# A transformer and state-space stack on one core: table clusters with longer products, and fewer slabs in two halves

## The chip, the cores and the metric

The kernel runs on one core of a Trainium2 chip. The metric is the device time of one execution in microseconds. Three runs of the kernel before took 3143.59 to 3145.2 us, with a median of 3145.1 us.

## The reference

The input is one sequence of 256 tokens of width 2048, in fp32. It goes through two blocks.

The first block has two layers. Each layer computes `h = rms_norm(x) * (1 + scale) + shift`, a token mixer (a chunkwise mLSTM beside a sliding-window attention, with an input projection and an output projection), and a squared-ReLU feed-forward:

```
def squared_relu_mlp(h, w_up, w_down):
    return jnp.square(jax.nn.relu(h @ w_up)) @ w_down
```

`w_up` is 2048 x 8192 and `w_down` is 8192 x 2048. Shift, scale and gate come from `silu(c) @ w_ada`, which has its own 2 x 2048 x 12288 weights.

The second block has a state-space layer (S5) and an attention layer with forget gates. The S5 layer needs tables that depend on its parameters alone: powers of the complex decay of every one of 128 groups of 16 channels with 64 states, multiplied with the output matrix C and the input matrix B. The scan over 256 tokens is then done four tokens at a time, with small matrices `C A^n B` inside the four. Those tables are computed while the second feed-forward of the first block runs.

## The kernel before, in words

**Slabs.** All large products are cut into slabs. A slab is 128 output columns of a weight matrix, 2048 x 128, or 1 MB of fp32, that is 16 chunks of 128 x 128. SyncE loads it into one of five raw buffers. ScalarE makes the high part of the weights (`WH`, rounded to fp32r), VectorE the low part (`WL`, the raw weights minus the high ones). The activations are kept in the same way as a high and a low part of 256 columns each.

TensorE's `slab` (from line 450) does 16 chunks of high weights and then 16 chunks of low weights:

- In **one-form** (the slab's number is in `ONE`, line 164) each chunk of high weights is multiplied with the high and with the low activations, as two products of 256 columns into the same 256 columns of the bank. With the 16 low products that makes 48 products of 256 columns. One instruction evicts the result.
- In **two-half form** nine of the 16 chunks (`WIDE`) take both activation parts in one product of 512 columns, into both halves of the bank. The others are as in one-form. That makes 23 high products (9 of them of 512 columns) and 16 low ones. ScalarE copies the second half out and VectorE adds the first to it.

`IN_TWO` (line 161) is a list of slabs which are taken out of `ONE`. Both forms compute the same sums. Results go to three banks in turn (`BANK_OF`).

**Order.** Every engine has its own program with its instructions in a fixed order, and semaphores join them. The slabs run in one sequence through the whole kernel. A slab waits for its high weights (`s_hi`), for its bank (`s_ev`), and between the high and the low products for its low weights (`s_free`).

**Feed-forward.** The feed-forward of a layer is 128 slabs, here counted from 0 to 127 from `J_MLP[l]` on: four times 16 up slabs and 16 down slabs. Slabs 0 to 2 (`SIDE`) are done apart, as plain fp32 products. In the kernel before, slabs 3 and 4 and the slabs 8, 24, 40, ..., 120 are in two halves in both layers. In the first layer VectorE also multiplies 82 tiles of `w_ada` during slabs 4 to 110. TensorE does nothing but slabs there.

**Table clusters.** In the second layer `s5_tables` (from line 758) puts small work on TensorE behind some slabs: six transposes behind slab 22, and twelve clusters behind slabs 40, 43, 46, 49, 56, 59, 62, 65, 72, 75, 78 and 81. A cluster is 32 fp32 products of 32 columns. They are grouped by `i` (four) and `ri` (the real, then the imaginary part), and in each group four products, `w` = 0 to 3, use four separate strips of 32 columns of the array. The trace shows every fp32 product as two instructions, so a cluster is a row of x64. ScalarE copies the first 128 columns of the bank out. The list `TABLES` (line 160) holds all thirteen places, and in the kernel before the two slabs behind each are in two halves.

Of the kernel before, what the change touches and what calls it, by code (L numbers as in the profile page):

```python
# [56 lines left out]
J_MLP = [53, N_LAYER + 53]  # L57
# [10 lines left out]
def down_slab(l, j, n):  # L68
    return J_MLP[l] + 32 * j + 16 + n
# [33 lines left out]
SIDE = 3  # L103
# [52 lines left out]
for _j in range(N_SLABS):  # L156
# [1 line left out]
    HI_AT.append(_n)  # L158
TAKEN = {_j for _t in TURNS[:-1] for _j in range(_t + 16, _t + 16 + SIDE)}
TABLES = [22] + [40 + 16 * _n + 3 * _g for _n in range(3) for _g in range(4)]  # L160
IN_TWO = ({J_MLP[_l] + _m for _l in range(2) for _m in [SIDE, SIDE + 1] + list(range(8, 128, 16))}
          | {J_MLP[1] + _m + _i for _m in TABLES for _i in (1, 2)}
          | {_t + _n for _t in (J_OUT[0], J_OUT[1], J_Z, J_GLU, J_Y2, J_Y3) for _n in (1, 6, 11)} | {J_OUT[1] + 2})
ONE = (set(range(RAMP)) | {_j for _l in range(2) for _j in range(J_OUT[_l] + 1, J_MLP[_l])}
       | {_j for _l in range(2) for _j in range(J_MLP[_l] + SIDE, J_MLP[_l] + 128)}
# [1 line left out]
       | set(range(J_Z + 2, J_GLU)) | set(range(J_GLU + 1, J_Y2 + 1)) | set(range(J_Y2 + 2, J_KV))  # L167
       | set(range(J_KV + 5, J_KV + 18)) | set(range(J_FOX + 23, J_Y3 + 1)) | set(range(J_Y3 + 2, N_SLABS))) - IN_TWO
DOWN = {down_slab(_l, _p, _n) for _l in range(2) for _p in range(4) for _n in range(16)}
# [26 lines left out]
def build(nc, d, out):  # L196
    ctx = ExitStack()
    with ctx:
# [34 lines left out]
        def m(name, shape, off, dt=F32):  # L233
            return at(name, shape, int(M + off * kb), dt)
# [78 lines left out]
        CC = m("cc", (64, 2, 32), 64)  # L313
        KST = m("kst", (16, 32), 62)
        CP = [m(f"cp{i}", (32, 16), 80 + 2 * i) for i in range(3)]
        BTG = m("btg", (4, 2, 128), 86)
# [109 lines left out]
        def tensor(e):  # L426
            release = {}

            def claim(b):

                if b in release:
                    e.wait_ge(release[b][0], release[b][1])
                return BK[b]

            def mm(o_, l_, r_, start, stop):
                return e.matmul(o_, l_, r_, start=start, stop=stop, skip_group_check=True)  # L436

            def tr(o_, i_):
                n = i_.shape[0]
                return e.transpose(o_, i_, ident[0:n, 0:n])  # L440
# [269 lines left out]
            def layer(l):  # L710
# [29 lines left out]
                for j in range(4):  # L740
                    for n in range(16):
                        if j or n >= SIDE:
                            slab(up_slab(l, j, n), hx, h_chunk(2 * l) if j == 0 and n == SIDE else None)
                        if l == 1:
                            s5_tables(32 * j + n)

                    def raised(k):
                        e.wait_ge(s_uh, 64 * l + 16 * j + k + 1)
                        e.wait_ge(s_ul, 64 * l + 16 * j + k + 1)

                    for n in range(16):
                        slab(down_slab(l, j, n), lambda k: HB[:, k, :, :], None if n else raised)
                        if l == 1:
                            s5_tables(32 * j + 16 + n)
# [3 lines left out]
            def s5_tables(m):  # L758

                if m == 22:  # L760
                    e.wait_ge(s_pd5, 4)
                    for b, cols in ((3, (cs, sn, a2r, a2i)), (4, (a3r, a3i))):
                        bank = claim(b)
                        for i, c in enumerate(cols):
                            last = tr(bank[0:64, 128 * i:128 * i + 128], c)
                        last.then_inc(s_att, 1)
                        release[b] = (s_atr, b - 2)
                for n in range(3):
                    for g in range(4):
                        if m == 40 + 16 * n + 3 * g:  # L770
                            u = 4 * n + g
                            bank = claim(3)
                            e.wait_ge(s_cb, n + 1)
                            e.wait_ge(s_bt, 16 * (u + 1))
                            for i in range(4):
                                for ri in range(2):
                                    for w in range(4):
                                        rows = slice(32 * w, 32 * w + 32)
                                        last = mm(bank[rows, 32 * i:32 * i + 32], BTG[:, i, ri, rows],
                                                  CC[:, 16 * g + 4 * i + w, ri, :], ri == 0, ri == 1)  # L780
                            last.then_inc(s_k0m, 1)
                            release[3] = (s_k0, u + 1)

# [2086 lines left out]
```

## Time and profile before

| | |
|---|---|
| median of three runs | 3145.1 us |
| span of the profiled execution, first to last instruction (the profile gives no other time of it) | 3145.5 us |
| TensorE products | 26577 instructions, busy 3075.0 us |
| TensorE weight loads | busy 2931.5 us |
| VectorE busy | 2404.3 us |
| ScalarE busy | 1529.5 us |
| mean granted TensorE clock | 0.992 |

Products overlap in the array. A product of 256 columns has a duration of about 0.28 us in the trace, but the next starts about 0.11 us later. So the time that a product costs is read from the distance between starts, and a row's "us" (from the first start to the last end of a group) is longer than the distance to the next row.

### The profile page before, as it was taken

Reading aid. Unit: us, or ns where it says so; the run is one execution under the profiler, and the core shown is the slowest. Engines: PE = TensorE matmul, PEld = TensorE weight load, DVE = VectorE, ACT = ScalarE, POOL = GpSimd, SP = SyncE. Lnnn points to the kernel's source line nnn. Section 1 sums busy time; section 2 is a strip of 40 time slices with the busy share of each in tenths; the row PEclk is TensorE's granted clock in tenths of the full one; section 3 lists DMA queues with packets and bytes.
Section 4 is the critical chain, followed back from the end, with each engine's and each line's share of the span. In section 5 each row is a group of like instructions: output and inputs, shape, how many; then the busy total and the mean of one; then the engine's idle time right before and its main releaser. Section 6 shows DMA issues by size and latency. Waiting matters only on the chain.

```text
span 3145.5 us, 61783 instructions
## 1 busy us (share of the span) xinstructions
PE 3075.0 (98%) x26577; PEld 2931.5 (93%) x26577; DVE 2404.3 (76%) x2964; ACT 1529.5 (49%) x2232; POOL 0.2 (0%) x4
## 2 busy tenths in 40 slices
PE   5999999999999999999999999999999999999999
PEld 3889999999999988989999999999899999999998
DVE  7898999788888788776887666687688767556764
ACT  2465664343434556666534444445433556434454
POOL 0000000000000000000000000000000000000000
PEclk7999999999999999999999999999999999999999
DMA  9888869999999745665688666895555554654453
GB/s 409 337 301 331 318 254 349 346 334 350 337 339 342 254 163 212 218 225 175 231 298 307 221 223 240 283 303 202 217 181 189 215 190 158 213 179 159 148 188 121
DMA packets 137025, 791.05 MB, mean 251 GB/s; under 512 B 20081, under 2 KB 38641, under 8 KB 46001
## 3 DMA queue, kind: packets, MB, share of 16 engines
q1 hardware_dynamic: 119714, 769.33, 67.2%
q10 hardware_dynamic: 17040, 17.76, 1.6%
q8 instruction: 211, 3.46, 0.4%
q14 instruction: 60, 0.49, 0.0%
HBM read 769.28 MB, written 17.76 MB: 250 GB/s over the span
## 4 chain that ended last, share of the span: by engine, by line
PE 53%; DVE 2%; ACT 1%; issue 0%; ACTq 0%; DVEq 0%
PE bk L436 52%; DVE wl L1649 1%; PE bk L440 0%; ACT wh L949 0%; DVE pr L1649 0%; DVE Hst L1649 0%; DVE xl L1649 0%; DVE ss L1649 0%; DVE qa L1657 0%; DVE p L1649 0%; DVE X L1649 0%; DVE raw L1657 0%; ACT ln L949 0%; DVE hg L1657 0%; ACT rsy L949 0%
## 5 line engine op out<-in xcount | busy, mean ns | idle before, releaser
L1649 DVE TENSOR_TENSOR wl<-raw,wh 128x2048 fp32r<-128x2048 f32 (+1 forms) x481 | 1092.5, 2271 | 321.1 <-ACT wh L949 318.1
L436 PE MATMUL bk<-HX,wh 128*128 128x256 f32 (+1 forms) x8058 | 1105.8, 294 | 1.8 <-ACT wh L949 1.6
L949 ACT ACTIVATE wh<-raw 128x2048 fp32r<-128x2048 f32 x477 | 911.8, 1912 | 351.1 <-PE bk L436 322.7
L436 PEld LDWEIGHTS bk<-HX,wh 128*128 128x128 f32 x8058 | 1022.2, 188 | 53.4 <-ACT wh L949 2.4
L436 PE MATMUL bk<-HX,wl 128*128 128x256 f32 x4560 | 569.0, 277 | 5.2 <-DVE wl L1649 5.2
L436 PEld LDWEIGHTS bk<-HX,wl 128*128 128x128 f32 x4560 | 542.3, 188 | 7.1 <-DVE wl L1649 7.0
L436 PE MATMUL bk<-hb,wh 128*128 128x256 f32 (+1 forms) x3916 | 488.0, 282 | 0.1
L436 PEld LDWEIGHTS bk<-hb,wh 128*128 128x128 f32 x3916 | 468.2, 188 | 8.2 <-issue 0.3
L1657 DVE SCALAR_TENSOR_TENSOR raw<-raw,cb 128x2048 f32<-128x2048 f32 x192 | 437.5, 2283 | 14.8 <-DMA raw<-in_w_ada 14.7
L436 PE MATMUL bk<-hb,wl 128*128 128x256 f32 x2048 | 253.8, 276 | 0.0
L436 PEld LDWEIGHTS bk<-hb,wl 128*128 128x128 f32 x2048 | 242.5, 188 | 0.0
L949 ACT ACTIVATE ur<-bk 128x256 f32<-128x256 f32 x122 | 46.8, 383 | 354.5 <-PE bk L436 338.4
L436 PE MATMUL bk<-sq,raw 128*128 128x257 f32 (+1 forms) x544 | 119.3, 379 | 0.0
L436 PEld LDWEIGHTS bk<-sq,raw 128*128 128x128 f32 x544 | 102.7, 189 | 17.4 <-issue 1.7
L949 ACT ACTIVATE yt<-bk 128x256 f32<-128x256 f32 x81 | 31.0, 383 | 164.8 <-PE bk L436 157.1
L436 PE MATMUL bk<-hf,rampw 128*128 128x256 f32 x256 | 65.6, 423 | 34.3 <-ACT hf L949 28.8
L436 PEld LDWEIGHTS bk<-hf,rampw 128*128 128x128 f32 x256 | 54.5, 215 | 45.4 <-issue 17.3
L1657 DVE SCALAR_TENSOR_TENSOR ur<-ur 128x256 f32<-128x256 f32 x122 | 51.6, 423 | 45.1 <-ACT ur L949 43.8
L1649 DVE TENSOR_TENSOR tacc<-tacc,ts 128x768 f32<-128x768 f32 (+1 forms) x84 | 72.5, 863 | 2.6 <-ACT yu L949 1.9
L436 PE MATMUL bk<-mx,wh 128*128 128x256 f32 (+1 forms) x483 | 64.8, 285 | 2.2 <-DVE mx L1649 2.1
L436 PE MATMUL bk<-ax,wh 128*128 128x256 f32 (+1 forms) x460 | 65.6, 294 | 0.1
L436 PEld LDWEIGHTS bk<-mx,wh 128*128 128x128 f32 x483 | 60.8, 188 | 4.7 <-ACT mx L949 2.1
(313 smaller groups left out, 2584.1 us busy)
## 6 DMA issues: line engine op xcount, KB each, us to landing
raw<-in_w_ada SPq DMA_DIRECT2D x192, 1024.0 KB, 6.9
raw<-in_w_up SPq DMA_DIRECT2D x128, 1024.0 KB, 6.5
raw<-in_w_down SPq DMA_DIRECT2D x128, 1024.0 KB, 5.7
raw<-in_w_in SPq DMA_DIRECT2D x66, 1024.0 KB, 5.3
raw<-in_kv_w SPq DMA_DIRECT2D x33, 1024.0 KB, 4.9
raw<-in_w_out SPq DMA_DIRECT2D x32, 1024.0 KB, 5.4
raw<-in_s_w_in SPq DMA_DIRECT2D x32, 1024.0 KB, 4.9
raw<-in_fox_w_in SPq DMA_DIRECT2D x32, 1024.0 KB, 4.8
```

The costliest lines, as they stand in the source:

```text
L436: return e.matmul(o_, l_, r_, start=start, stop=stop, skip_group_check=True)
L949: return e.activation(o_, i_, f, **kw)
L1649: return e.tensor_tensor(o_, a_, b_, op)
L1657: return e.scalar_tensor_tensor(o_, a_, s_, b_, op0, op1, accum_out=sums)
```

## The change

Two things are changed. In each of the twelve table clusters the four products of the last group's real part (`i == 3`, `ri == 0`) get `PAST[u]` more columns, 0 to 16, where `u` is the number of the cluster. The added columns are read from the imaginary part, which lies next in `CC`, and are written into columns of the bank that nobody reads.

`IN_TWO` gets shorter. In the first feed-forward slabs 8, 24, ..., 120 are no longer in two halves (slabs 3 and 4 still are). In the second feed-forward slabs 40, 56, 72 and 88 and the two slabs behind each of the twelve clusters are no longer in two halves. Slabs 3, 4, 8, 23, 24, 104 and 120 stay. So 8 and 28 slabs change to one-form.

```
 TABLES = [22] + [40 + 16 * _n + 3 * _g for _n in range(3) for _g in range(4)]
-IN_TWO = ({J_MLP[_l] + _m for _l in range(2) for _m in [SIDE, SIDE + 1] + list(range(8, 128, 16))}
-          | {J_MLP[1] + _m + _i for _m in TABLES for _i in (1, 2)}
+PAST = [0, 1, 2, 3, 4, 5, 6, 7, 8, 10, 12, 16]
+IN_TWO = ({J_MLP[_l] + _m for _l in range(2) for _m in [SIDE, SIDE + 1]}
+          | {J_MLP[1] + _m for _m in [*range(8, 40, 16), 104, 120]}
+          | {J_MLP[1] + TABLES[0] + _i for _i in (1, 2)}
           | {_t + _n for _t in (J_OUT[0], J_OUT[1], J_Z, J_GLU, J_Y2, J_Y3) for _n in (1, 6, 11)} | {J_OUT[1] + 2})
...
                                         rows = slice(32 * w, 32 * w + 32)
-                                        last = mm(bank[rows, 32 * i:32 * i + 32], BTG[:, i, ri, rows],
-                                                  CC[:, 16 * g + 4 * i + w, ri, :], ri == 0, ri == 1)
+                                        n_ = 32 + (PAST[u] if i == 3 and ri == 0 else 0)
+                                        cc = CC[:, 16 * g + 4 * i + w, :, :].rearrange("p r n -> p (r n)")
+                                        last = mm(bank[rows, 32 * i:32 * i + n_], BTG[:, i, ri, rows],
+                                                  cc[:, 32 * ri:32 * ri + n_], ri == 0, ri == 1)
```

## Rows read from the trace of the kernel before

**Rows 1.** The page: busy time of each engine, and the chain that ended last.

```profile
PE 3075.0 (98%) x26577; PEld 2931.5 (93%) x26577; DVE 2404.3 (76%) x2964; ACT 1529.5 (49%) x2232; POOL 0.2 (0%) x4
...
PE 53%; DVE 2%; ACT 1%; issue 0%; ACTq 0%; DVEq 0%
```

**Rows 2.** Busy by stretch: us, PE, PEld, DVE, ACT, POOL (x), PEclk, DMA, GB/s.

```profile
487.93:1140.90 652.97, 652.97 (x5690) 650.00 (x5689) 534.20 (x501) 283.97 (x287) 0.00 (x0) 1.00 0.87 322
1717.92:2079.31 361.39, 361.39 (x3591) 348.54 (x3589) 242.62 (x261) 158.76 (x165) 0.00 (x0) 1.00 0.74 251
2128.88:2168.45 39.57, 39.57 (x338) 39.57 (x337) 30.57 (x31) 21.21 (x28) 0.00 (x0) 1.00 0.58 199
```

**Rows 3.** Timeline of TensorE, second feed-forward: start us, us, operation, [idle before].

```profile
1970.49 3.79 PE L436 MATMUL bk<-hb,wh 128*128 128x256 f32 x32
...
1992.25 3.81 PE L436 MATMUL bk<-hb,wh 128*128 128x512 f32 x23
```

**Rows 4.** Timeline of TensorE, second feed-forward, last down slabs.

```profile
2128.88 3.93 PE L436 MATMUL bk<-hb,wh 128*128 128x256 f32 x32
2132.64 2.05 PE L436 MATMUL bk<-hb,wl 128*128 128x256 f32 x16
...
2168.45 3.82 PE L436 MATMUL bk<-hb,wh 128*128 128x512 f32 x23
```

**Rows 5.** Timeline of TensorE, first feed-forward, slabs 5 to 8.

```profile
473.66 2.15 PE L436 MATMUL bk<-HX,wl 128*128 128x256 f32 x16 [0.30 <-DVE wl L1649]
476.51 4.04 PE L436 MATMUL bk<-HX,wh 128*128 128x256 f32 x32 [0.70 <-ACT wh L949]
480.39 2.05 PE L436 MATMUL bk<-HX,wl 128*128 128x256 f32 x16
...
487.93 3.82 PE L436 MATMUL bk<-HX,wh 128*128 128x512 f32 x23
491.59 1.98 PE L436 MATMUL bk<-HX,wl 128*128 128x256 f32 x16
```

**Rows 6.** Timeline of TensorE, first slab of the S5 output projection.

```profile
2559.42 0.47 PE L436 MATMUL bk<-go,wh 128*128 128x256 f32 x2 [0.84 <-DVE go L1649]
2559.73 2.05 PE L436 MATMUL bk<-go,wl 128*128 128x256 f32 x16
```

**Rows 7.** Timeline of TensorE, third and fourth table cluster.

```profile
1758.27 0.76 PE L436 MATMUL bk<-cc,btg 128*32 128x32 f32 x64
1758.96 4.01 PE L436 MATMUL bk<-HX,wh 128*128 128x512 f32 x23
...
1764.70 3.82 PE L436 MATMUL bk<-hb,wh 128*128 128x512 f32 x23
...
1770.17 3.79 PE L436 MATMUL bk<-hb,wh 128*128 128x256 f32 x32
...
1775.70 0.76 PE L436 MATMUL bk<-cc,btg 128*32 128x32 f32 x64
```

**Rows 8.** Timeline of TensorE, behind the sixth table cluster.

```profile
1833.08 3.92 PE L436 MATMUL bk<-hb,wh 128*128 128x512 f32 x23
1836.84 1.98 PE L436 MATMUL bk<-hb,wl 128*128 128x256 f32 x16
```

**Rows 9.** Timeline of TensorE, third stage, slabs between state products.

```profile
2421.78 4.04 PE L436 MATMUL bk<-HX,wh 128*128 128x256 f32 x32
...
2427.63 0.86 PE L436 MATMUL bk<-u,ks 32*32 32x192 f32 x24
...
2429.45 3.90 PE L436 MATMUL bk<-HX,wh 128*128 128x256 f32 x32
...
2435.09 0.86 PE L436 MATMUL bk<-u,ks 32*32 32x192 f32 x24
```

**Rows 10.** Timeline of TensorE, first layer: 16 plain fp32 products of 256 columns.

```profile
223.50 7.07 PE L436 MATMUL bk<-hf,raw 128*128 128x256 f32 x32
230.41 0.82 PE L440 MATMUL bk<-cst,ta 128*128 128x128 f32 x6
```

## The prediction

> **What bounds the kernel now.** The page comes first: TensorE is busy for 98% of the span and holds 53% of the chain that ended last, with VectorE at 2% and ScalarE at 1% [rows 1]. The busy times by stretch come next: in the first feed-forward (487.93 to 1140.90) TensorE is busy for 652.97 of 652.97 us at the full granted clock (2.4 GHz), VectorE for 534.20 and ScalarE for 283.97 [rows 2]; in the stretch of the table clusters (1717.92 to 2079.31) it is busy throughout as well. So the question is not what waits, but how far apart TensorE starts its products.
>
> That is read from the timeline of TensorE. A slab is one row "wh" (high products) and one row "wl" (16 low products); the distance between two "wh" starts is the slab's time. In one-form (48 products of 256 columns) there are two distances and nothing between them, called the short and the long pace below (and a slab, or a cluster's exit, is short or long by the pace that it runs at or leaves). Short: 1970.49 to 1992.25 is four slabs, 5.44 us each, 113.3 ns a product; the rows read 3.79 and 1.98 [rows 3, 5]. Long: 2128.88 to 2168.45 is seven slabs, 5.653 us each, 117.8 ns a product; the rows read 3.93 and 2.05 [rows 4]. The granted clock is 1.00 in the stretch of long pace as in the others, so this is not the throttle [rows 2]. The price of the long pace is 0.213 us a slab.
>
> The pace is kept until something changes it, and the timeline shows what does:
> - A stop inside a one-form slab leaves it at the long pace. In the first feed-forward slab 5 waits 0.30 us for its low half and slab 6 0.70 us for its high half; the low half of slab 6 then reads 2.05 [rows 5]. The second feed-forward repeats this, and a wait of 0.84 us at 2559.42 is followed by 2.05 too [rows 6]. I count ten slabs of this form with such a stop in the trace; all ten go on at the long pace.
> - A two-half slab (its row is 128x512, x23) ends it: slab 8 at 487.93 has a low half of 1.98 [rows 5], and the one at 2168.45 ends the long pace [rows 4]. At the short pace such a slab takes 5.46 to 5.47, 0.02 to 0.03 more than one-form.
>
> **The change part by part.**
>
> *First feed-forward, slabs 8, 24, ..., 120 go to one-form.* Slabs 3 and 4 stay two-half, but the stops in slabs 5 and 6 come behind them, so slab 8 is the one that restores the pace today. Nothing ahead of it changes: the same loads, high and low halves and waits end at the same times, so slab 8 is reached at the long pace. From there to the end of the stage TensorE never stops today [rows 2], it runs no products but the slabs', and a TensorE that runs later makes stops rarer. I find nothing that would end the long pace: the most slabs in a row at the long pace without a stop or a two-half slab in the trace are the seven between 2128.88 and 2168.45 (and the slab of the stop ahead of it), ended only by the two-half slab [rows 4]. Sum: 120 slabs of 5.653 is 678.4 us, against 652.97 now [rows 2]: +25.4 us. If the pace were short anyway: 120 of 5.44 is 652.8, -0.2 us. These are the two ends; I take the first, its stops and its recovery both being rows of this very place.
>
> *The evictions of the 36 slabs that change form (8 and 28).* One-form needs one eviction where two-half needs a ScalarE copy and a VectorE add. That frees some 0.4 us of ScalarE a slab and costs nothing: both engines have slack in the stretch [rows 2], and a bank is reused three slabs, over 16 us, later. Were that cover gone, a late eviction would be a stop of a few tenths. No instruction waits on anything new, and no load, high or low half changes its place in a queue, SP's included.
>
> *Table clusters.* In slabs 40 to 103 of the second feed-forward twelve clusters stand, three slabs apart, with seven slabs behind the fourth and the eighth, and twenty-two (to the two-half slab 104 that stays) behind the last: 63 slabs that run at the pace that the cluster before them leaves. Today: 361.39 us for the 64 slabs [rows 2]. One cluster's pattern is 0.69 us for the cluster (1758.27 to 1758.96), 5.74 for the two-half slab behind it, at the long pace, 5.47 for the second two-half slab, short again, and 5.53 for the slab ahead of the next cluster, 0.09 over 5.44 [rows 7]. Ten of twelve exits are of this kind; the first and the sixth (3.76 us from 1833.08 to 1836.84, low half 1.98, so 5.57) come out short [rows 8]. So today the clusters' aftermath costs 10 x 0.33 + 2 x 0.16 + 4 x 0.02 (slabs 40, 56, 72, 88) = 3.7 us over 64 x 5.44 + 12 x 0.78 = 357.5; the sum, 361.2, meets the window within 0.2.
>
> After: exits go into one-form slabs. What such an exit costs is seen behind the state product of the third stage: a long exit is 5.85 us (2421.78 to 2427.63), a short one 5.64 (2429.45 to 2435.09), both with 0.09 ahead of the next cluster [rows 9], so 0.10 for the entry and the pace on top. The longer products: a column of an fp32 product of 256 takes 6.91 / 16 / 256 = 1.69 ns (223.50 to 230.41) [rows 10]; the twelve lengths sum to 74 columns, four products side by side, so 74 x 1.69 ns = 0.13 us in all. Base: 357.5 + 12 x 0.10 + 0.13 = 358.8. To it comes 0.213 for every slab behind a long exit.
> - All short: 358.8, -2.5 us. All long: 358.8 + 63 x 0.213 = 372.3, +10.9 us.
> - Whether 1.7 to 27 ns more at the cluster's end turn an exit, no row says. For long: 10 of 12 exits today, and of 27 one-form slabs that come behind products of another kind 24 read long. For short: rows 9 hold one kind of cluster with two different exits, so small shifts do decide. I take nine of twelve long, nearest to these counts: 47 slabs, 10.0 us, +7.5 us.
>
> Two rules of the Trainium skill stand against this, and the sums above do without them. "TensorE: Matmul & The Clock Gate", section "Back-to-back issue gap", gives a gap of N/2.4 + 2.5 ns: 109 ns at 256 columns and 216 at 512, whatever ran before. By it removing a two-half slab loses 9 x 2.5 ns and the first feed-forward would change by +0.2 us in place of +25.4; the trace shows two paces at one size and one clock, 113.3 and 117.8 ns [rows 3, 4], so I weigh it only as the rival without memory. "TensorEngine Tiling (Array Packing)", section "Instruction Overhead", says that a free dimension of 1 costs as much as one of 60. By it 33 to 48 columns are the same as 32 and the exits stay as today's, about 10 of 12 long; the fp32 row's 1.69 ns a column [rows 10] is no test of sizes that small.
>
> **Sum.** +25.4 + 7.5 = +32.9 us. The profiled execution has a span of 3145.5 us, 0.4 over the median of the three runs, 3145.1; the differences are between stretches of this one execution and are put on the median: 3178.0 us.
>
> **Rivals.**
> 1. Most clusters exit short (up to a third long), the first feed-forward stays long: +25.4 and -2.5 to +4: 3168 to 3174. For it: the two short exits today. Against: 24 of 27.
> 2. The pace heals by itself. This is the one on the other side. Its place is slab 8: if the long pace lasts only some slabs behind a stop, and no two-half slab is needed, the first feed-forward gives -0.2 us and the clusters -2.5 to +4: 3142.5 to 3149, not slower. It decides as long as fewer than 6.3 / 0.213 = 30 of the 183 slabs at stake are long. Against it: seven full slabs of unchanged 5.653 us [rows 4].
> 3. The first feed-forward short (slab 5's or 6's stop lands differently and slab 7 is short already), the clusters long: -0.2 and +7.5 to +10.9: 3152 to 3156. Against: ten stops of ten.
> 4. Something turns the pace midway through the first feed-forward, say where up goes over to down products: about +12.7 and +7.5: 3165.
>
> **How the numbers follow.** Forecast (first feed-forward long throughout, half or more of the clusters long, 3174 to 3182): 0.60. Rival 1: 0.20. Rival 2: 0.09. Rival 3: 0.07. Rival 4: 0.04. A difference under 0.2%, 6.3 us, can't be told from none here. Slower: 0.60 + 0.20 + 0.07 + 0.04 = 0.91; same: 0.08 of rival 2; faster: 0.01 of it. The range 3162 to 3184 holds the forecast, rivals 1 and 4 and the bounds of the cluster term, 3168.0 and 3181.4, with some 2.5 us for a new stop at the upper end. Its lower end stops short of rivals 2 and 3.
>
> **What would show it.** Right: from slab 8 at 487.93 on the low rows read 2.04 or 2.05, high rows 3.93, starts 5.653 apart, up to the stage's sums about 25 us later than 1140.90; slabs 5 to 7 as today. Behind each cluster the pace is one of the two and stays it to the next cluster. Slab 104 restores it. Wrong: rows of 1.98 behind 487.93 in one-form; a third pace, or a pace that drifts; a long slab that turns short with no two-half slab, stop or cluster between; or the time moving in another stage, since nothing outside these two stretches should change by over 0.3 us.

## The result, and the profile of the changed kernel

The changed kernel takes 3188.4 us (median; 3189.2, 3189.6, 3187.6, and one execution of 3160.3), the kernel before 3145.2 beside it: ratio 1.0117, interval 1.0097 to 1.0137. It is slower, as forecast, but by 43 us and not by 33, and so 4.4 us above the upper end of the range, 3184. The ratio counts all four executions, the low one too: by it the changed kernel takes about 3182 us, which is inside the range.

The profiled execution has a span of 3187.4 us against 3145.5, +41.9. On the page TensorE is busy for 38.6 us more [rows 1], with 324 more products (9 for each of the 36 slabs that changed form) and as many weight loads:

```profile
PE 3113.6 (98%) x26901; PEld 2984.1 (94%) x26901; DVE 2390.1 (75%) x2929; ACT 1524.0 (48%) x2215; POOL 0.2 (0%) x4
```

Where it went, by stretches between the starts of the blocks of sums of squares (sq, raw), in us:

| stretch | before | changed | difference | forecast |
|---|---|---|---|---|
| start to first block | 436.7 | 434.0 | -2.7 | 0 |
| first feed-forward | 708.5 | 733.95 | +25.4 | +25.4 |
| mixer of the second layer | 347.2 | 347.3 | +0.1 | 0 |
| second feed-forward | 723.86 | 735.05 | +11.2 | +7.5 |
| third stage | 430.7 | 438.6 | +7.9 | 0 |
| fourth stage, to the end of the span | 498.5 | 498.5 | 0 | 0 |

*First feed-forward.* Timeline of TensorE, slabs 5 to 8 (beside [rows 5]):

```profile
470.93 2.08 PE L438 MATMUL bk<-HX,wl 128*128 128x256 f32 x16 [0.28 <-DVE wl L1653]
473.79 4.04 PE L438 MATMUL bk<-HX,wh 128*128 128x256 f32 x32 [0.78 <-ACT wh L953]
477.66 2.04 PE L438 MATMUL bk<-HX,wl 128*128 128x256 f32 x16
...
485.20 3.93 PE L438 MATMUL bk<-HX,wh 128*128 128x256 f32 x32
488.97 2.05 PE L438 MATMUL bk<-HX,wl 128*128 128x256 f32 x16
```

The stops are those of before, slab 8 keeps the long pace, and the last slab of the stage, 670 us later, still has it. Slab 127's low half, and behind it the products that sum the columns:

```profile
1161.72 2.05 PE L438 MATMUL bk<-hb,wl 128*128 128x256 f32 x16
1163.60 0.59 PE L438 MATMUL bk<-tacc,ones 128*128 128x256 f32 x2
```

From 485.20 to 1163.60 it is 678.40 us for 120 slabs, 5.653 each; the forecast's product was 678.4.

*Table clusters.* The first cluster, and the end of the stretch at slab 104:

```profile
1740.83 3.79 PE L438 MATMUL bk<-HX,wh 128*128 128x256 f32 x32
1744.45 1.98 PE L438 MATMUL bk<-HX,wl 128*128 128x256 f32 x16
1746.36 0.76 PE L438 MATMUL bk<-cc,btg 128*32 128x32 f32 x64
1747.05 4.04 PE L438 MATMUL bk<-HX,wh 128*128 128x256 f32 x32
1750.93 2.05 PE L438 MATMUL bk<-HX,wl 128*128 128x256 f32 x16
1752.81 3.93 PE L438 MATMUL bk<-HX,wh 128*128 128x256 f32 x32
...
2111.31 2.05 PE L438 MATMUL bk<-HX,wl 128*128 128x256 f32 x16
2113.19 3.82 PE L438 MATMUL bk<-HX,wh 128*128 128x512 f32 x23
```

The stretch is entered at the short pace; the first exit is long, and so are the other eleven. From 1740.83 to 2113.19 it is 372.36 us, the forecast's all-long bound (372.3). Slab 104 restores.

*Third stage.* The waits that the profile puts down to "issue" (it names no engine and no DMA that released them), before and then changed:

```profile
2453.98 0.44 PE L436 MATMUL bk<-Hst,raw 128*32 128x64 f32 x17 [0.25 <-issue]
...
2457.80 0.29 PE L436 MATMUL bk<-u,ks 32*32 32x64 f32 x2 [0.78 <-issue]
...
2461.35 0.64 PE L436 MATMUL bk<-Hst,raw 128*32 128x64 f32 x28 [0.75 <-issue]
...
2465.17 0.52 PE L436 MATMUL bk<-u,ks 32*32 32x128 f32 x13 [0.70 <-issue]
...
2466.65 4.92 PE L436 MATMUL bk<-HX,wh 128*128 128x512 f32 x23
```

```profile
2488.34 1.22 PE L438 MATMUL bk<-u,ks 32*32 32x192 f32 x20 [1.82 <-issue]
...
2495.96 0.32 PE L438 MATMUL bk<-Hst,raw 128*32 128x64 f32 x7 [0.64 <-issue]
...
2499.85 1.00 PE L438 MATMUL bk<-Hst,raw 128*32 128x64 f32 x57 [0.72 <-issue]
...
2506.32 0.80 PE L438 MATMUL bk<-Hst,raw 128*32 128x64 f32 x18 [3.88 <-issue]
2507.05 6.47 PE L438 MATMUL bk<-HX,wh 128*128 128x512 f32 x23
```

In place of 2.5 us TensorE stands for 7.1 us in the batch of eight state products, and its granted clock is lower behind the stop of 3.88 us. By stretch (columns as in [rows 2], PEclk the third from the end):

```profile
2506.32:2510.00 3.68, 3.68 (x27) 3.12 (x27) 2.85 (x6) 1.52 (x3) 0.00 (x0) 0.50 1.03 430
```

0.50 is 1.2 GHz, and the next high half takes 6.47 us for 4.92. The waits' 4.6 and this 1.5 are 6.1 of the 7.9 us; the rest I can't assign row by row.

The -2.7 us lies ahead of the first block, where the two kernels have the same instructions. That stretch took 433.8 to 436.7 us over all the kernels below, so it is the spread of single executions.

### The profile page after: what moved, and what is told of

Same layout as the page of the kernel before. It is cut to its first block, busy times and chain, and to the rows that moved or that the text cites. A ratio compares the mean times of both kernels' runs of the same rounds, so it can differ in the third digit from the quotient of the medians.

```text
span 3187.4 us, 62354 instructions
## 1 busy us (share of the span) xinstructions
PE 3113.6 (98%) x26901; PEld 2984.1 (94%) x26901; DVE 2390.1 (75%) x2929; ACT 1524.0 (48%) x2215; POOL 0.2 (0%) x4
## 4 chain that ended last, share of the span: by engine, by line
PE 52%; DVE 2%; ACT 1%; issue 1%; DMA 0%; ACTq 0%; DVEq 0%
PE bk L438 52%; DVE wl L1653 1%; PE bk L442 0%; ACT wh L953 0%; DMA raw<-in_w_up 0%; DVE pr L1653 0%; DVE Hst L1653 0%; DVE xl L1653 0%; DVE ss L1653 0%; DVE qa L1661 0%; DVE p L1653 0%; DVE X L1653 0%; DVE raw L1661 0%; ACT ln L953 0%; DVE hg L1661 0%
## 5 line engine op out<-in xcount | busy, mean ns | idle before, releaser
L438 PE MATMUL bk<-HX,wh 128*128 128x256 f32 (+1 forms) x8229 | 1118.6, 292 | 1.6 <-ACT wh L953 1.5
L438 PEld LDWEIGHTS bk<-HX,wh 128*128 128x128 f32 x8229 | 1042.1, 188 | 45.8 <-ACT wh L953 2.4
L438 PE MATMUL bk<-hb,wh 128*128 128x256 f32 (+1 forms) x4069 | 500.8, 280 | 0.1
L438 PEld LDWEIGHTS bk<-hb,wh 128*128 128x128 f32 x4069 | 487.1, 188 | 1.7 <-issue 0.3
L438 PE MATMUL bk<-hb,wl 128*128 128x256 f32 x2048 | 260.3, 279 | 0.0
L1653 DVE TENSOR_TENSOR y<-bk,y 128x256 f32<-128x256 f32 x66 | 28.0, 424 | 66.4 <-PE bk L438 64.0
```

Source lines behind the costliest of these rows:

```text
L1653: return e.tensor_tensor(o_, a_, b_, op)
```

## The experiments

Each median stands beside the kernel before on the same chip (medians of 3144.1 to 3145.7 us). A stretch's length is of the one profiled execution.

**1. Second feed-forward's part alone**: the changed kernel, the first feed-forward's two-half slabs put back.

```
+          | {J_MLP[0] + _m for _m in range(8, 128, 16)}
```

> The change, but the first feed-forward keeps its eight two-half slabs. Theory (the pace is kept until a two-half slab ends it): the first feed-forward takes 652.97 us from slab 8 on as before, the table stretch 361.4 + 11.0 us; 3156.2 us if nothing else moves. In the changed kernel the third stage took 8 us more than before (stops between the state products, and a clock of half speed behind the last). Theory A: that comes with the time at which the stage is reached, by chance of the execution, and is not tied to either part: here anything from 0 to 8 us. Theory B: it belongs to the second feed-forward's part: then 8 us here too, 3164. Rival without memory of the pace: 3145 and no low row of 2.05 in the table stretch.

Measured: 3155.8 us, 1.004 (1.0025 to 1.0055). First feed-forward 708.5, as before; third stage 432.4, so 1.7 us more and not 8. Second feed-forward 730.8: the first five exits are short, the sixth, the first whose product is five columns longer, is long, and all behind it:

```profile
1811.71 0.76 PE L439 MATMUL bk<-cc,btg 128*32 128x32 f32 x64
1812.40 3.90 PE L439 MATMUL bk<-hb,wh 128*128 128x256 f32 x32
1816.14 1.98 PE L439 MATMUL bk<-hb,wl 128*128 128x256 f32 x16
...
1828.92 0.77 PE L439 MATMUL bk<-cc,btg 128*32 128x32 f32 x64
1829.62 4.03 PE L439 MATMUL bk<-hb,wh 128*128 128x256 f32 x32
1833.49 2.05 PE L439 MATMUL bk<-hb,wl 128*128 128x256 f32 x16
```

**2. First feed-forward's part alone**: the kernel before, with its eight slabs one-form.

```
-IN_TWO = ({J_MLP[_l] + _m for _l in range(2) for _m in [SIDE, SIDE + 1] + list(range(8, 128, 16))}
+IN_TWO = ({J_MLP[_l] + _m for _l in range(2) for _m in [SIDE, SIDE + 1]}
+          | {J_MLP[1] + _m for _m in range(8, 128, 16)}
```

> The kernel before, but slabs 8, 24, ..., 120 of the first feed-forward go to one-form; the table stretch is as before. Theory: 120 slabs of 5.653 in place of 5.44 us, +25.4 us, 3170.5 us, in executions where slab 7 is at the long pace; an execution in which the stops of slabs 5 and 6 leave the short pace would be at 3145. Theory B on the third stage: no more than before there; theory A: 0 to 8 us more. Rival (evictions of the one-form slabs are what costs): gaps between slabs, and products still 113.3 ns apart.

Measured: 3174.5 us, 1.0067 (1.0034 to 1.0101); four executions from 3174.4 to 3177.5, two of 3152.4 and 3148.6. In the profiled one the first feed-forward takes 733.96, and the third stage 436.5, where no slab had been changed. The two lower times are less by about the 25 us of a first feed-forward at the short pace; no trace of them was taken, so that reading is an inference.

**3. The lengths set to nothing**: the changed kernel with `PAST = [0] * 12`.

> The change with all twelve added lengths set to 0: the clusters end as before, the forms of the slabs are the changed kernel's. Theory (the lengths move the start of the next slab but do not decide its pace): same as the changed kernel within 0.3 us in the two stretches, all or nearly all exits long. Rival (the lengths matter): the exits differ from those with lengths, and the first cluster, whose length was 0 in both, is the only one sure to be the same.

Measured: 3172.9 us, 1.0093 (1.0078 to 1.0108). All twelve exits are short, where nearly all were expected long:

```profile
1741.45 3.79 PE L438 MATMUL bk<-HX,wh 128*128 128x256 f32 x32
1745.08 1.98 PE L438 MATMUL bk<-HX,wl 128*128 128x256 f32 x16
1746.99 0.76 PE L438 MATMUL bk<-cc,btg 128*32 128x32 f32 x64
1747.68 3.90 PE L438 MATMUL bk<-HX,wh 128*128 128x256 f32 x32
1751.41 1.98 PE L438 MATMUL bk<-HX,wl 128*128 128x256 f32 x16
...
2100.33 2.90 PE L438 MATMUL bk<-HX,wh 128*128 128x512 f32 x16
```

From 1741.45 to 2100.33 it is 358.88 us, the forecast's all-short bound (358.8). But the first cluster of the changed kernel has length 0 too, with the same instructions ahead of it and the same short pace into it, and its exit is long. So what decides there is neither the length nor the pace that TensorE comes with, but something that differs between executions.

**4. The lengths alone**: the kernel before, its clusters' last products lengthened as in the change.

> The kernel before with the added lengths alone, all two-half slabs kept. Theory: +0.1 us, nothing that can be told from 3145.1. Rival (the lengths turn exits): where a length makes the first two-half slab behind a cluster short, 0.17 us each, at most 10 x 0.17 = 1.7 us less; the rows of the low half behind each cluster read 1.98 or 2.05 and tell which.

Measured: 3145.3 us, 1.0003 (0.9993 to 1.0012): the lengths behind two-half slabs do nothing that can be measured. All twelve exits of this execution are short, lengths or not.

**5. Only slab 8 stays two-half in the first feed-forward** (before; slabs 24, 40, ... 120 one-form).

```
+IN_TWO = ({J_MLP[_l] + _m for _l in range(2) for _m in [SIDE, SIDE + 1, 8]}
+          | {J_MLP[1] + _m for _m in range(8, 128, 16)}
```

> The kernel before, but in the first feed-forward only slab 8 stays in two halves, slabs 24 to 120 go to one-form. Theory on the pace: slab 8 alone does all the work there, the first feed-forward stays at 652.8 us from slab 8 on (it was 653.0). Theory on the third stage (TensorE's program is fetched in blocks of 16 KB, 256 instructions, and where the block's edges fall in the state products decides how long they stop): 63 products more, so 126 instructions more, shift the edges by 126 of 256, close to the 144 and 136 (modulo 256) of the two kernels that stopped long, so the third stage takes 436 to 439 us in place of 430.7 though no slab is at the long pace: 3151 us. Rival (the third stage's 6 to 8 us come with the long pace or the later time): 430.7 us and 3145.

Measured: 3152.8 us, 1.002 (1.0011 to 1.003). The first feed-forward takes 708.4 us, no more than before: one two-half slab behind the last stop does the work of all eight.

```profile
483.17 2.05 PE L437 MATMUL bk<-HX,wl 128*128 128x256 f32 x16
485.05 3.82 PE L437 MATMUL bk<-HX,wh 128*128 128x512 f32 x23
488.71 1.98 PE L437 MATMUL bk<-HX,wl 128*128 128x256 f32 x16
```

Yet the kernel is slower, and all of that is the third stage: 438.2 us, with 8.2 us of "issue", the longest:

```profile
2468.25 0.64 PE L437 MATMUL bk<-Hst,raw 128*32 128x64 f32 x13 [4.07 <-issue]
```

**6 and 7. Nothing but a shift**: the kernel before with small products, whose result nobody reads, at its very start: 36 in one (144 instructions more on TensorE's queue, what eight slabs add) and 16 in the other (64).

```
+            for _ in range(36):
+                mm(BK[3][:, 480:512], ONES[:, 0:128], ONES[:, 0:32], True, True)
```

> The kernel before with 36 small fp32 products (144 instructions) added at the very start, where TensorE waits for the input anyway; their result goes unused. Theory of the block edges: third stage 436 to 439 us, as where 144 instructions were added by eight slabs of one-form; 3151 us. Rival: 430.7 and 3145 us.

> The same with 16 small products, 64 instructions. Theory of the block edges: a third stage between or beside the two values, 428 to 439 us; if the stops are set by the edge alone it differs from 430.7 by more than the 0.5 us that two kernels with equal positions differed. Rival: 430.7.

Measured: 3149.4 us, 1.0013 (1.0004 to 1.0022), third stage 438.2; and 3146.2, 1.0002 (0.9992 to 1.0011), third stage 435.3. No slab has another form, and the third stage's loss is there. In the first:

```profile
2467.03 0.86 PE L436 MATMUL bk<-Hst,raw 128*32 128x64 f32 x22 [4.34 <-issue]
```

The page of before has a queue that fits such a stop. Third part, DMA queues (packets, MB, share):

```profile
q8 instruction: 211, 3.46, 0.4%
```

3.46 MB in 211 packets is 16.4 KB each. TensorE's 53,154 products and weight loads by 211 packets are 252 for one, and the changed kernel, with 648 more, has 214 packets. The traces tie the stops to this queue: in all fourteen, every "issue" stop of over 0.2 us in this batch ends 1.2 to 1.6 us behind the end of one of its packets. In before the four stops end at 2453.98, 2457.80, 2461.35 and 2465.17, the last packets ahead of them at 2452.59, 2456.42, 2459.96 and 2463.81, and from stop to stop it is 254, 252 and 254 products and weight loads. So each stop is a wait for the next block of instructions. Taken as blocks of 256, the lengths of the third stage, over all kernels, order by how far the instructions ahead of it are shifted:

| shift, modulo 256 | third stage, us |
|---|---|
| 0 (before, 4, 11) | 430.7, 430.2, 430.7 |
| 2 (12) | 430.0 |
| 28 (10) | 430.9 |
| 64 (7) | 435.3 |
| 118 (8), 126 (5) | 436.3, 438.2 |
| 136 (changed, 3, 9) | 438.6, 437.5, 436.3 |
| 144 (2, 6) | 436.5, 438.2 |
| 248 (1) | 432.4 |

A shift of 504 to 540 instructions (1 and 10) costs 0 to 2 us, one of 64 to 144 costs 4.5 to 7.5: where the block's edge falls decides, not how much was added.

**8. One two-half slab in the middle**: the changed kernel with slab 64 of the first feed-forward two-half.

> The changed kernel with slab 64 of the first feed-forward in two halves. Theory (the pace is kept until a two-half slab): long from slab 6 to 63, short from 64 on, so 64 slabs x 0.213 = 13.6 us less than the changed kernel in that stage, 720.4 us from sum to sum in place of 733.9. The table clusters: if the class of an exit is set at the last stop ahead of them and kept, all exits of n = 0 in one execution are alike; the first cluster's exit (added length 0) is long or short by the execution, and once long the rest stays long: 720.9 to 735.1 us for the second feed-forward. Rival (pace heals or is set by the engines' load): no jump at slab 64.

Measured: 3173.6 us, 1.0086 (1.007 to 1.0103). First feed-forward 720.3, 13.6 less than the changed kernel for 64 slabs of 0.213 = 13.6:

```profile
796.25 3.93 PE L438 MATMUL bk<-hb,wh 128*128 128x256 f32 x32
800.02 2.05 PE L438 MATMUL bk<-hb,wl 128*128 128x256 f32 x16
801.91 3.82 PE L438 MATMUL bk<-HX,wh 128*128 128x512 f32 x23
805.57 1.98 PE L438 MATMUL bk<-HX,wl 128*128 128x256 f32 x16
```

The second feed-forward takes 734.9 us; all twelve exits are long again.

**9. The changed kernel once more**, for a second trace of the same instructions.

> The changed kernel once more, for a second trace. Theory: its terms come back one by one: 733.9 us for the first feed-forward from sum to sum (or 708.5 in an execution where slab 5's and slab 6's stops leave the short pace), 720.9 to 735.1 for the second, 436 to 439 for the third stage because the position of its instructions is the same. Rival (the 8 us of the third stage were chance of one execution): 430.7.

Measured: 3184.1 us, 1.0124 (1.011 to 1.0138). Third stage 436.3. Second feed-forward 730.3 in place of 735.1: the first five exits are short, from the sixth (five columns) on they are long as in the first experiment, but for the eleventh, whose first product came 190 ns behind the cluster's last instead of 123. And the first feed-forward has a surprise. It leaves the stop at the short pace, and loses it two slabs later, with no wait reported:

```profile
473.75 3.90 PE L438 MATMUL bk<-HX,wh 128*128 128x256 f32 x32 [0.70 <-ACT wh L953]
...
482.92 1.98 PE L438 MATMUL bk<-HX,wl 128*128 128x256 f32 x16
484.74 3.95 PE L438 MATMUL bk<-HX,wh 128*128 128x256 f32 x32
488.52 2.05 PE L438 MATMUL bk<-HX,wl 128*128 128x256 f32 x16
```

The high half that reads 3.95 holds one distance of 135 ns between two products; then it is long to the end of the stage.

**10. Into the clusters at the long pace**: lengths 0, the first feed-forward as before, and in the second no two-half slab between 8 and 104.

```
+PAST = [0] * 12
+          | {J_MLP[1] + _m for _m in [8, 104, 120]} | {J_MLP[0] + _m for _m in range(8, 128, 16)}
```

> All added lengths 0, the first feed-forward as before, and in the second no two-half slab between 8 and 104 (so 23 and 24 are one-form too). The six transposes behind slab 22 left the first two-half slab long in the kernel before. Theory (a cluster that is entered at the long pace is left at it; entered at the short pace it can go either way): long from slab 23 to 103, 81 slabs x 0.213 = 17.3 us over 81 of 5.44, 720.9 + 17.3 + some 0.2 = 738 us for the second feed-forward and 3159 + third stage 0 to 2 us. Rival (each exit is decided by the cluster alone, so that lengths of 0 come out short as in the run with lengths zero): long from 23 to 40 at most, short from 41 on, 725 us.

Measured: 3148.3 us, 1.0016 (1.0006 to 1.0025), second feed-forward 725.8, the rival's 725. The idea that a cluster passes on the pace that it is entered with falls at once:

```profile
1717.02 3.93 PE L437 MATMUL bk<-HX,wh 128*128 128x256 f32 x32
1720.79 2.05 PE L437 MATMUL bk<-HX,wl 128*128 128x256 f32 x16
1722.76 0.76 PE L437 MATMUL bk<-cc,btg 128*32 128x32 f32 x64
1723.45 3.90 PE L437 MATMUL bk<-HX,wh 128*128 128x256 f32 x32
1727.19 1.98 PE L437 MATMUL bk<-HX,wl 128*128 128x256 f32 x16
```

Exits 1 to 9 are short, the tenth (14 ns late, 140 in place of 126 behind the cluster) and eleventh long, the twelfth short again with its first product on time (126 ns).

**11. Two-half slabs right behind the stops**: the kernel before, slab 7 in place of 8 in both feed-forwards and 113 in place of 120 in the second.

```
+ [SIDE, SIDE + 1, 7] + list(range(24, 120, 16)) + [(120, 113)[_l]]
```

> A version meant to beat both: the kernel before with slab 7 in two halves in place of slab 8 in both feed-forwards, and slab 113 in place of 120 in the second. The number of instructions ahead of the third stage is the same, so the block edges there are where they were. Theory: slab 7 at the short pace twice, 2 x 0.2, and 113 to 119 short, 7 x 0.213 less: -1.9 us, 3143.6. Rival (a two-half slab directly behind a stop does not end the long pace): no gain at 113, or a loss of 1.7 where 120 is missed.

Measured: 3143.4 us, 0.9996 (0.9987 to 1.0005). The second feed-forward takes 720.5 us, against 722.4 with all exits short in experiment 5, for 8 slabs of 0.213 = 1.7. The rows agree: slab 112 is long, slab 113 and those behind it are short. But the time can't be told from that of before, and before's forms reach nearly the same by themselves: in experiment 7 the stop in slab 112 (0.10 us) left the short pace, and the second feed-forward took 720.8.

**12. The same, and the slabs ahead of the state products too**: slabs 7 to 14 of the third stage's projection two-half, and 32 of the small products at the start, which undo the shift (128 - 126 = +2).

> The same, and in the third stage the seven one-form slabs behind a state product in two halves as well; 32 small products at the start put the 126 instructions that this takes away back, so the block edges move by 2 instructions only. Theory: a long exit of 5.85 us becomes 5.70: 7 x 0.15 less, -3.0 us in all against before, 3142.6. Rival (VectorE, which has the scan there, is late with the added halves): stops in that stage, no gain or a loss.

Measured: 3140.8 us, 0.9991 (0.9982 to 1.0000), the lowest median here, though its interval ends at 1. The projection ahead of the batch takes 231.0 us for 232.1, and the third stage 430.0 in place of 430.7. That is some 1 to 2 us, in a profiled execution of 3143.4. The rest of the 3.3 us between the medians (3140.8 and 3144.1) is not shown to come from the slabs: the seven executions of 3139.4 to 3141.2 have a mean granted clock of 0.994 to 0.996, the other four (3143.4 to 3144.3) 0.993 like before. Experiment 6, with small products and no slab changed, has 0.995 in five of ten executions, where none of before is over 0.994. No run has these slabs without the small products.

## Why the prediction was right in its sign and too low

**First feed-forward, +25.4: right to the tenth**, mechanism and size. Alone it costs the same 25.4 (experiment 2). Rivals 2 and 4 fall: 120 slabs in a row keep the long pace, over the change from up to down products too, and a two-half slab ends it wherever it stands (5, 8). Rival 3's premise, a short slab 7, is not the usual case, but it occurs: in two of fourteen traces (9 and 10) slab 6's stop left the short pace, and in the second feed-forward in four (2, 3, 10 and 11). In 9 it gained next to nothing (733.55 us), since slab 8 lost the pace again. The one execution of 3160.3 us, 28 less than the median, is about what a first feed-forward at the short pace throughout would give; no trace shows it. "Ten stops of ten" was a count within one execution, whose stops are not independent.

**Evictions and queues: nothing, right.** VectorE and ScalarE do less, and from 485.20 to the sums TensorE does not stop.

**Table clusters, +7.5 forecast, +11.2 measured: the right mechanism, a term sized too small.** Both bounds were met, 372.36 for 372.3 and 358.88 for 358.8, in two kernels whose first clusters are alike. The step that failed is the count, "nine of twelve long": it took exits for independent draws, and they come in runs of one kind. With length 0 throughout, one execution has all twelve short (3; so have 2, 5, 6, 7, 11 and 12 with before's slabs behind the clusters, and 4 with the lengths besides), and another ten of twelve long (before), its two exceptions where the first product came 192 and 164 ns behind the cluster's last in place of 126.

That looks as if something were set ahead of the clusters and carried through them; no run shows what. A late first product alone doesn't decide. In the executions with long exits (before, 9) the three late ones (164 to 192 ns) came out short and the next was long again; in those with short exits ten late ones (134 to 205 ns, in 2, 4, 6, 11 and 12) stayed short and one (140 ns, in 10) came out long. Where the exits are short and one-form slabs follow, the exit turned at the product that is five columns longer, in both traces that have this (1 and 9). So the term is 11.2 us in one execution and 6.5 in another (730.3 - 723.86); that the second lies near the forecast's 7.5 is luck, with six of twelve exits long. Its baseline moves too: before's 723.86 is itself a poor draw, by some 1.4 us against 722.4. Rival 1 needed most exits short: it is what experiment 3 shows without the lengths, not the changed kernel.

The lengths were priced at 0.13 us and take 0.08: the cluster lasts 693 or 694 ns up to 4 columns, 700 at 5, 704 at 10, 712 at 16. The Trainium skill, "TensorEngine Tiling (Array Packing)", section "Instruction Overhead", has free dimensions up to some 60 cost the same. For 32 to 36 columns the trace agrees; beyond, 37 to 48 cost 4 to 19 ns a cluster (1 and changed), and the exits did not "stay as today's".

**Third stage, 0 forecast, +7.9 measured: a missing term.** "Nothing outside these two stretches should change by over 0.3 us" is the sentence that failed. A small state product takes 17 to 36 ns of TensorE's time (64 in 1.10 us, 24 in 0.86), and there the fetch of instructions, one packet for some 250 instructions, doesn't keep up: before already stood for 2.5 us. A change of 648 instructions moves the batch against the blocks' edges. Experiments 5, 6 and 7 show it, 6 and 7 without one slab changed. Why most edges cost under 1 or 2 us and the last one, in seven traces, 3.5 to 4.3 stays open. The waits marked "issue" in the trace of before were the sign, and I read past them.

**The sum by its own steps:** +25.4 for the first feed-forward as forecast, +11.2 for the clusters (3.7 over the forecast), +7.9 for the third stage, -2.6 of scatter ahead and between, together the span's +41.9. Less the third stage's 7.9 the median is 3180.5, within the range: the larger miss is this term, the smaller the clusters'.

**Left open:** what a stop does that makes TensorE go on at one pace or the other, and what makes the exits of one execution alike. No run controls it; only that a two-half slab clears it for the slabs behind is shown. That the two low times of experiment 2 are executions with a short first feed-forward is not shown either.

## What to carry to other kernels

Read the distance between starts of like instructions on the bound engine, not its busy share: here 98% busy held two paces 4% apart, and one slab of another form right behind the last stop is all that keeps the shorter one. Don't count outcomes of one trace as independent; take a second trace of the same kernel before a frequency becomes a term. And when an edit changes the number of instructions, look for the stretch of small instructions further on: its "issue" waits can move with the block edges, and a pad that nobody reads tells that apart from the edit itself, as long as the granted clock is compared too.

## What the runs showed of the hardware

- Products of 256 columns with a weight load each start 113.3 or 117.8 ns apart at the same granted clock, for 120 slabs if nothing comes between. The Trainium skill, "TensorE: Matmul & The Clock Gate", section "Back-to-back issue gap", gives N/2.4 + 2.5 ns, 109 at 256 columns, and calls it the gap of a product by itself; it has no gap that depends on what ran before. Neither pace agrees with 109, and by it the first feed-forward would have lost next to nothing.
- A delay of 14 or 22 ns in one distance (140 ns for 126 behind a cluster, 135 for 113 once in a slab) stood where the long pace began, in 10 and 9; the same 140 ns behind the last cluster of experiment 6, ahead of a two-half slab, left the short pace. In none of these traces did a one-form slab go back without a cluster, a stop or a two-half slab.
- Instruction blocks of 16.4 KB are fetched for TensorE, and runs of small products outrun them: the stops end 1.2 to 1.6 us behind a packet and last up to 4.3 us; in before none is over 0.8.
- Behind a stop of 3.88 us the granted clock was 0.50 (1.2 GHz), and the high half there took 6.47 us for 4.92. Behind before's last stop, 0.70 us, the clock stayed at 1.00.
